# One fp32 product per key chunk for turn and scores, and an earlier start of the last column sums, in a hybrid trunk step on one core

## What is computed

```python
def retention_chunk(R, inp):
    scores = jnp.einsum('bhtd,bhsd->bhts', q, k) * decay
    inner = jnp.einsum('bhts,bhse->bhte', scores, v)
    out = inner + cross[:, :, None] * jnp.einsum('bhtd,bhde->bhte', q, R)
    R_new = jnp.exp(lg * L)[:, None, None] * R + jnp.einsum('hs,bhsd,bhse->bhde', tail, k, v)
...
def mlstm_chunk(carry, inp):
    s = jnp.einsum('bhtd,bhsd->bhts', q, k) * w
...
y_prompt = rms_norm(hp, g_final)
y_sample = rms_norm(hs, g_final)
```

## Time and profile before

| | |
|---|---|
| median of 3 runs | 1048.03 us (1047.66 to 1048.28) |
| the profiled execution | 1047.74 us |
| its span, first to last instruction | 1046.0 us |
| TensorE busy | 1033.6 us, 99% |
| VectorE busy | 791.3 us, 76% |
| ScalarE busy | 515.1 us, 49% |
| GpSimd busy | 215.8 us, 21% |
| mean granted TensorE clock | 0.997 |
| HBM traffic | 133 GB/s over the span |

### The profile page before, as it was taken

One profiled execution on the slowest core, in us unless ns is written; L12 is line 12 of the kernel. 1 busy time (PEld: TensorE's weight loads), 2 busy tenths in 40 slices (PEclk: granted clock), 3 DMA queues, 4 the chain that ended last, 5 costly groups with the idle time before them and its releaser, 6 DMA issues.

```text
span 1046.0 us, 20867 instructions
## 1 busy us (share of the span) xinstructions
PE 1033.6 (99%) x8229; PEld 1025.3 (98%) x8229; DVE 791.3 (76%) x1497; ACT 515.1 (49%) x943; POOL 215.8 (21%) x190
## 2 busy tenths in 40 slices
PE   9999999999999999999999999999999999999996
PEld 8999999999999999999999999999999999999996
DVE  5985689997899986555755556588568899789996
ACT  6453366644666664433232223445336664466654
POOL 1100221212122111310332223210012222221210
PEclk9999999999999999999999999999999999999998
DMA  7447787878878466445354223543777888887852
GB/s 226 115 80 181 173 178 167 181 171 174 179 163 172 100 136 137 79 65 84 65 81 76 68 79 62 142 91 86 177 162 165 172 175 170 178 178 167 175 107 97
DMA packets 217051, 142.13 MB, mean 136 GB/s; under 512 B 8685, under 2 KB 214677, under 8 KB 216825
## 3 DMA queue, kind: packets, MB, share of 16 engines
q1 hardware_dynamic: 160824, 110.98, 40.3%
q0 software_dynamic: 56048, 29.79, 22.3%
q10 hardware_dynamic: 80, 0.02, 0.0%
HBM read 135.80 MB, written 3.29 MB: 133 GB/s over the span
## 4 chain that ended last, share of the span: by engine, by line
PE 92%; DVE 3%; issue 2%; DMA 2%; ACT 1%; SPq 0%; DVEq 0%; ACTq 0%
PE dense L887 41%; PE dense L763 35%; PE core_banks L887 6%; PE core_banks L763 3%; PE dense L833 1%; PE core_banks L1118 1%; PE core_banks L1103 1%; DMA sum_ident<-sq 1%; PE core_banks L1121 1%; PE core_banks L1093 1%; DMA x_tok<-in_x_prompt 1%; DVE h_op L1811 1%; DVE w_lo L1769 1%; DVE h_raw L1799 0%; PE core_banks L1130 0%
## 5 line engine op out<-in xcount | busy, mean ns | idle before, releaser
L1306 ACT ACTIVATE w_hi<-w_src 128x512 fp32r<-128x512 f32 x182 | 113.2, 628 | 97.8 <-PE dense L887 55.7
L1306 ACT ACTIVATE w_hi<-w_raw 128x512 fp32r<-128x512 f32 x182 | 112.4, 629 | 77.6 <-PE dense L887 52.1
L887 PE MATMUL dense<-h_op,w_hi 128*128 128x272 f32 x768 | 147.8, 291 | 0.8 <-DVE h_op L1811 0.8
L1769 DVE TENSOR_TENSOR w_lo<-w_src,w_hi 128x512 fp32r<-128x512 f32 x182 | 124.6, 689 | 29.9 <-ACT w_hi L1306 28.1
L1769 DVE TENSOR_TENSOR w_lo<-w_raw,w_hi 128x512 fp32r<-128x512 f32 x182 | 123.9, 688 | 29.0 <-ACT w_hi L1306 27.0
L763 PE MATMUL dense<-xg_hi,w_hi 128*128 128x272 f32 x672 | 141.6, 292 | 0.0
L763 PE MATMUL dense<-xg_hi,w_lo 128*128 128x272 f32 x672 | 138.4, 288 | 0.0
L763 PE MATMUL dense<-xg_lo,w_hi 128*128 128x272 f32 x672 | 138.1, 287 | 0.0
L887 PE MATMUL dense<-x_late_hi,w_hi 128*128 128x272 f32 x432 | 125.7, 291 | 0.0
L887 PE MATMUL dense<-x_op_hi,w_lo 128*128 128x272 f32 x432 | 124.6, 288 | 0.0
L887 PE MATMUL dense<-x_late_hi,w_lo 128*128 128x272 f32 x432 | 124.5, 288 | 0.0
(11 more groups left out here) (363 smaller groups left out, 2389.4 us busy)
## 6 DMA issues: line engine op xcount, KB each, us to landing
w_raw<-in_w_ffn_up SPq DMA_DIRECT2D x43, 512.0 KB, 5.0
w_src<-in_w_ffn_gate SPq DMA_DIRECT2D x36, 512.0 KB, 5.2
w_raw<-in_w_in SPq DMA_DIRECT2D x31, 512.0 KB, 8.4
w_src<-in_w_ffn_gate POOLq DMA_DIRECT2D x36, 256.0 KB, 5.5
w_raw<-in_w_ffn_up POOLq DMA_DIRECT2D x36, 256.0 KB, 6.0
w_src<-in_w_ffn_down SPq DMA_DIRECT2D x16, 512.0 KB, 5.3
w_raw<-in_w_ffn_down SPq DMA_DIRECT2D x16, 512.0 KB, 5.2
w_raw<-in_w_ffn_down SPq DMA_DIRECT2D x16, 384.0 KB, 5.8
```

What stands on the lines that cost most here:

```text
L887: last = nc.tensor.matmul(out, w[:, k, :], x, start=o in OPENS and k == 0 and m == 0, stop=k == KH - 1 and m == 2, skip_group_check=o not ...
L1306: nc.scalar.activation(block_of(w_hi, n, o), source(e, o), ACT.Copy).then_inc(block_hi, 1)
L1769: nc.vector.tensor_tensor(block_of(w_lo, n, o), source(g % 2, o), block_of(w_hi, n, o).bitcast(F32), ALU.subtract)\
```

## The change

In `step_scores` the four transposes of the keys and the four score products become four products of 256 columns: the stationary operand is the key chunk, the moving operand a view of two pieces of 128 columns, the query chunk and a second identity `ident_near` that POOL fills next to `proj`. The results lie in banks 0 and 1 of `X`, per chunk 128 score columns and 128 turned key columns; the values go to bank 3. VectorE reads the scores and the keys with a stride, and in the retention heads it, not ScalarE, now makes `k_tail`. Small tables of the mixer are put into one allocation.

In the last pair `turn_last(0)` and `sum_last(0)` are issued ahead of the wait for `down_taken` of block 6. `add_last(2)` on VectorE is gone: `sum_old` adds the column sums of the older squares and tile 7 (chunks 2, 3, sample) ahead of the last quarter of block 6, and `sum_last(1)` adds those of tile 6 onto the same PSUM columns.

```diff
-        proj = sb("proj", [P, 2, 4, T])
+        proj_wide = sb("proj_wide", [P, 2 * (2 * 4 * T + P) - 3 * T])
+        proj = proj_wide[:, 0:2 * 4 * T].rearrange("p (n a t) -> p n a t", n=2, a=4)
+        ident_near = proj_wide[:, 2 * 4 * T:2 * 4 * T + P]
...
+        def query_and_ident(h, c):
+
+            q = (h % 2) * 4 * T + SLOT[0] * T + c * P
+            stride = 2 * 4 * T - q
+            return proj_wide[:, q:q + 2 * stride].rearrange("p (a s) -> p a s", a=2)[:, :, 0:P]
+
+        KEY_CHUNKS = X[:, 0:2, :].rearrange("p a b -> p (a b)").rearrange("p (c a d) -> p c a d", c=NC, a=2)
+        SCORES_OF, KEYS_OF = KEY_CHUNKS[:, :, 0, :], KEY_CHUNKS[:, :, 1, :]
...
+                    if o == 6 and g == 2 * STEPS - 1:
+                        turn_last(0)
+                        sum_last(0)
                     if o in before:
                         pe.wait_ge(down_taken, BLOCKS * D + order_of(g).index(before[o]) + 1)
                     if o == 1 and n and c == 2 and d >= 2:
                         pe.wait_ge(out_taken, 2 * d - 2)
-                    if o == 6 and g == 2 * STEPS - 1:
-                        turn_last(0)
-                        sum_last(0)
                     pe.wait_ge(block_lo, BLOCKS * g + o + 1)
                     if o == 6 and g == 2 * STEPS - 1:
                         part(o, range(last_k))
                         turn_last(1)
+                        sum_old()
                         part(o, range(last_k, KH)).then_inc(product_done, 1)
...
-                pe.wait_ge(last_summed, step + 1)
+                if step:
+                    pe.wait_ge(last_squared, 5)
+                else:
+                    pe.wait_ge(last_summed, 1)
                 for c in END_CHUNKS[step]:
-                    last = nc.tensor.matmul(final_sum(c), sq_last[:, 0, CH[c]], ones[:, 0:1], start=True, stop=True)
+                    last = nc.tensor.matmul(final_sum(c), sq_last[:, 0, CH[c]], ones[:, 0:1], start=step == 0, stop=True,
+                                            skip_group_check=step == 1 and c != END_CHUNKS[1][0])
...
+            def sum_old():
+
+                pe.wait_ge(last_squared, 4)
+                for c in END_CHUNKS[1]:
+                    nc.tensor.matmul(final_sum(c), sq_last[:, 1, CH[c]], ones[:, 0:1], start=c == END_CHUNKS[1][0], stop=False,
+                                     skip_group_check=c != END_CHUNKS[1][0])
...
+                if h == 0:
+                    pe.wait_ge(mixer_consts, 1)
                 for c in range(NC):
-                    nc.tensor.transpose(X[:, 0, CH[c]], p(h, 1, CH[c]), ident[:, :])
+                    nc.tensor.matmul(KEY_CHUNKS[:, c, :, :], p(h, 1, CH[c]), query_and_ident(h, c), start=True, stop=True)
                 for c in range(NC):
-                    nc.tensor.transpose(X[:, 1, CH[c]], p(h, 2, CH[c]), ident[:, :])
+                    nc.tensor.transpose(X[:, 3, CH[c]], p(h, 2, CH[c]), ident[:, :])
                 nc.tensor.transpose(X[:, 2, 0:P], sample_block(h, 1), ident[:, :])
                 nc.tensor.transpose(X[:, 2, P:2 * P], sample_block(h, 2), ident[:, :])
-                for c in range(NC):
-                    nc.tensor.matmul(X[:, 3, CH[c]], p(h, 1, CH[c]), p(h, 0, CH[c]), start=True, stop=True)
...
-                if h == H:
-                    act.wait_ge(table_loaded, 16)
-                if h >= H:
-
-                    nc.scalar.activation(k_tail[:, 0:NC, :], X[:, 0, :].rearrange("p (c d) -> p c d", c=NC), ACT.Copy,
-                                         scale=table[:, TAIL + h - H:TAIL + h - H + 1])
...
                     last_square(DT - 2, 1)
-                    add_last(2, sq_last[:, 1, :])
                     take_last(2)
...
-                    nc.vector.tensor_tensor(scores[:, 0:TP], X[:, 3, :], weights[:, 0:TP], ALU.mult)
+                    nc.vector.tensor_tensor(grid(scores[:, 0:TP]), SCORES_OF, grid(weights[:, 0:TP]), ALU.mult)
...
-                    nc.vector.tensor_tensor(k_tail[:, 0:NC, :], grid(X[:, 0, :]), keep, ALU.mult)
+                    nc.vector.tensor_tensor(k_tail[:, 0:NC, :], KEYS_OF, keep, ALU.mult)
...
-                    nc.vector.tensor_tensor(grid(scores[:, 0:TP]), grid(X[:, 3, :]), decay.broadcast_to([P, NC, P]), ALU.mult)
+                    nc.vector.tensor_tensor(grid(scores[:, 0:TP]), SCORES_OF, decay.broadcast_to([P, NC, P]), ALU.mult)
...
+                    nc.vector.tensor_scalar(k_tail[:, 0:NC, :], KEYS_OF, table[:, TAIL + h - H:TAIL + h - H + 1], None, ALU.mult)
...
+            link(nc.gpsimd.memset(ident_near[:, :], 0.0))
+            link(triangle(ident_near[:, :], [[-1, P]], ALU.not_equal, 1.0))
             link(nc.gpsimd.memset(sel[:, :, :], 1.0))
```

More of the change, by code:

```diff
@@ L304, in hybrid_trunk_step @@
         at["next"] = y_ret_end
-        proj = sb("proj", [P, 2, 4, T])
+        proj_region = at["next"]
+        proj_wide = sb("proj_wide", [P, 2 * (2 * 4 * T + P) - 3 * T])
+        proj = proj_wide[:, 0:2 * 4 * T].rearrange("p (n a t) -> p n a t", n=2, a=4)
+        ident_near = proj_wide[:, 2 * 4 * T:2 * 4 * T + P]
+        at["next"] = proj_region + (2 * 4 * T + P) * 4
         table = sb("table", [P, tables.shape[1]])
@@ L334, in hybrid_trunk_step @@
         mask = sb("mask", [P, P])
[L335 to L340, removed]
+        tables_of = {}
+        minis = sb("minis", [P, (NC + 1) * (3 * H + 15)])
+        first = 0
+        for name, inner in (("key_col", H), ("neg_m_exp", H), ("stats", 6), ("mean_var", 2)):
+            tables_of[name] = minis[:, first:first + (NC + 1) * inner].rearrange("p (c a) -> p c a", a=inner)
+            first += (NC + 1) * inner
+        for name, outer in (("m_prev_all", H), ("small", 7)):
+            tables_of[name] = minis[:, first:first + (NC + 1) * outer].rearrange("p (a c) -> p a c", a=outer)
+            first += (NC + 1) * outer
+        key_col, neg_m_exp, m_prev_all = (tables_of[name] for name in ("key_col", "neg_m_exp", "m_prev_all"))
+        stats, mean_var, small = (tables_of[name] for name in ("stats", "mean_var", "small"))
         mixer_end = at["next"]
@@ L1590, in step_values @@
                     act.wait_ge(mixer_consts, 1)
-                if h == H:
-                    act.wait_ge(table_loaded, 16)
-                if h >= H:
-                    nc.scalar.activation(k_tail[:, 0:NC, :], X[:, 0, :].rearrange("p (c d) -> p c d", c=NC), ACT.Copy,
-                                         scale=table[:, TAIL + h - H:TAIL + h - H + 1])
-                nc.scalar.activation(v_tok[:, 0:NC, 0:P], X[:, 1, :].rearrange("p (c d) -> p c d", c=NC), ACT.Copy)\
+                nc.scalar.activation(v_tok[:, 0:NC, 0:P], X[:, 3, :].rearrange("p (c d) -> p c d", c=NC), ACT.Copy)\
                     .then_inc(v_ready, 1)
@@ L2058, in add_last @@
             def add_last(m, other):
-                cols = END_COLS[m // 2]
+                cols = END_COLS[0]
                 if m == 1:
@@ L2063, in add_last @@
                 else:
-                    dve.wait_ge(last_squared, 2 if m == 0 else 5)
+                    dve.wait_ge(last_squared, 2)
                 nc.vector.tensor_tensor(sq_last[:, 0, cols], sq_last[:, 0, cols], other[:, cols], ALU.add)\
```

## The result

Over 12 runs each the median went from 1048.05 us (1047.30 to 1050.33) to 1050.52 us (1049.83 to 1052.71). The ratio is 1.0025, with a 95% interval of 1.0018 to 1.0033: +2.6 us, from +1.9 to +3.5 (the medians themselves lie 2.5 apart). The forecast was +3.1 us, 1051.1, inside a range of 1049.6 to 1052.4. The profiled execution of the changed kernel took 1050.80 us with a span of 1049.1, against 1047.74 and 1046.0. In the experiments the median of the kernel before leaves out one execution of 1251.18 us, in which the mean granted clock was 0.752.

A forecast was written before the change was run, and what follows sets the result against it. The prediction took TensorE, busy 1033.6 of 1046.0 us, to bound the kernel. The mixer's +3.2 us and the end's -0.1 us summed to +3.1 us, giving 1051.1 us, range 1049.6 to 1052.4.

The forecast's parts named there:

- TensorE bounds the mixer: Mixer, 410 to 622 us: TensorE busy 212.00 of 212.00 us, so its gains or losses go straight into the end.
- The price of 256 columns, 0.217 us, and +3.2 us: Key products in the mixer: eight instructions at 0.217 us, 1.73 against 1.33 us a head, +3.2 us over 8 heads.
- The floor: TensorE instructions with one moving column take 0.107 us each, near the 0.111 us of 128 columns.
- the rival: Key products in the mixer: 256 columns cost 0.111 us as 128 do, giving 1044.4 us; chance 0.08.
- The rest of the mixer, nothing: Value transposes, `k_tail` on VectorE, strided reads and POOL's constants in the mixer: all covered, costed at nothing.
- the slack of 1.7 us: Last head: VectorE's chain ends 1.7 us ahead of TensorE's state update; forecast to become 1.0 us, at no cost.
- The end, -0.1 us: Last pair: VectorE's unbroken queue sets when block 6 is taken; only a wait at the last sums goes, -0.1 us.
- The sum: Whole kernel: +3.2 us from the mixer and -0.1 us from the end, +3.1 us, giving 1051.1 us.
- an instruction costs by its number: Mixer: pitch set by loading 128 weight columns, not the stream; -3.5 - 0.1, 1044.4 us; chance 0.08.
- the end gives up to 1.7 us: End: if TensorE's wait and `add_last(2)` held the chain, up to 1.7 us comes off, 1049.5 us; chance 0.06.
- VectorE is late for the state update: Retention heads: VectorE's longer chain delays `step_updates`, part of 2.8 us; within the slower case, 1052 to 1054 us, chance 0.06.
- the view in two pieces costs more: Key products: the jumping moving view raises the mixer's cost to 4.1 us; within the slower case, chance 0.06.

The follow-up runs named there:

- mixer_only: Changed kernel with its end part put back as before, leaving the mixer part alone; 1050.57 us against 1047.89 for the kernel before, ratio 1.0030.
- ktail_dve: Kernel before with only the scaled keys of the retention heads moved from ScalarE to VectorE; 1047.51 us against 1047.89, ratio 0.9993.
- cols192: Changed kernel with 96 query and 96 identity columns, not 128 each, in key products of heads 1 to 7; 1047.43 us, kernel before 1047.89.
- end_move_only: Kernel before with only the last pair's first turns and sums moved ahead of the wait for block 4; 1047.98 us in a single execution.
- end_only: Kernel before with the three changes of the end and the mixer untouched; 1047.85 us against 1047.89, ratio 1.0009.
- end_sums_only: Kernel before with older squares summed by TensorE and VectorE's last addition gone, turns not moved; 1049.04 us in a single execution.

## Why the prediction was right, step by step

**TensorE bounds the mixer.** Right: PE busy 212.00 of 212.00 us before and after, no wait of PE in the mixer in the changed kernel, mixer_only and ktail_dve, and every change of the pitch came out in the tail.

**The price of 256 columns, 0.217 us, and +3.2 us.** Right: 0.216, 1.73 us a head, +0.40 a head. It was read from four instructions of another stage that happened to have 272 columns. The floor, with which the rival argued, is real but a floor only: cols192 lies well above it at 0.163.

**The rest of the mixer, nothing.** Right for time on TensorE: the slack of 1.7 us became about 1.0, and nobody waited. But a term was left out. Moving four instructions to VectorE shifted everything behind them in its stream, and a gap of 0.40 us that VectorE had at the end, on the chain of waits, became 0.04: -0.36 us. The forecast had this gap in its own rows, the 0.46 us of idle time in the first line of the earlier trace rows, and passed over it: it called VectorE's queue from there on unbroken and did not ask what stood ahead of it, since nothing in the change seemed to touch it.

**The end, -0.1 us.** Right in kind, small in size by half: the end part alone gave -0.2 in the tail. The mechanism was as forecast in the main: VectorE's queue sets when block 6 is taken, all but 0.06 us of it. What was undersized is the last sums, 0.51 us in the chain for six instructions against 0.64: the forecast had a gain "up to 0.15 if the weight load slips under the turn", and that is what came. What was missed are the 0.06 us at the taking of block 6. The forecast called VectorE's queue unbroken there, but its copy at 1037.04 started as TensorE's turns ended, so the turns' move gave it a little (end_move_only). Its start of 1034.87 for the first sums is the turns' start with their pitch added, and not a row; the trace has 1034.92, which changes nothing in the sum.

**The sum.** 3.2 - 0.36 - 0.2 = +2.6 us; the tails say 642.0 - 639.3 = +2.7 and 641.9 - 639.3 = +2.6, and 12 runs each +2.6. Of the forecast of +3.1 the term of 3.2 held and two small gains were missed or undersized. That what the forecast passed over was small against the 3.2 is luck: it had given no reason why the gap on VectorE should stay. The first pair of profiles alone, with +3.1 us of span, agreed with the forecast better than it should have: 0.4 us of it was the start of that execution.

**The rivals.** That an instruction costs by its number is refuted by the row of 256 columns and by cols192. That the end gives up to 1.7 us is refuted by end_only and end_move_only. That VectorE is late for the state update is refuted by ktail_dve, and that the view in two pieces costs more by the pitch of 0.216 us, below the row of 272 columns in one piece.

## What to carry to other kernels

Fewer instructions are no gain on a TensorE that is busy streaming: count moving columns times passes, as long as that lies above the floor (0.107 us for a single column here). A turn made as 128 more columns of a plain fp32 product is streamed in both of its instructions, 0.21 us against 0.11 for a transpose, and the weight load that it saves was already hidden. For differences under 1 us measure from a landmark behind the noisy part; two profiles of one kernel differed by 1.3 us in span and by less than 0.1 from the landmark on. And look at the granted clock at the other end: where it fell before the last products were through, it added 0.1 and 0.4 us (cols192, end_move_only) that no edit had put there.

## What was not expected of the hardware

VectorE's gap of 0.40 us between two instructions, with nothing to wait for in the profile, stands in the same place (0.39 to 0.40 us) in every profile of the kernel before, end_only, end_move_only and end_sums_only, and is 0.04 us in every profile of those that have four more instructions on VectorE earlier, useful or not (7 profiles; 5 of the others). So a change on an engine can win or lose some 0.4 us at a place that it does not touch. What the engine does in this gap is not shown by any row; that it fetches its instructions is a guess that was not tested.

The loss of the same size on TensorE (0.41 us in the last sums of end_move_only) is another thing: there the granted clock was 0.50. In the other executions it fell to 0.50 only as the last sums ended or later, in cols192 while they ran.
